# Outer weight sums of a seven-product matrix product: made by adding transfers instead of VectorE, with two waits and three signs moved

## What is computed

```
for i in 0, 1:
    x = x + 0.5 * swiglu_ffn(rmsnorm(x, n_ffn1[i]), ffn1_w_gu[i], ffn1_w_down[i])
    h = rmsnorm(x, n_mix[i])
    x = x + (gla_mixer(h, ...) if i == 0 else pool_mixer(h, ...))
    x = x + mem_cross_attn(rmsnorm(x, n_xattn[i]), rmsnorm(mem, n_mem[i]), x_w_q[i], x_w_kv[i], x_w_o[i])
    x = x + 0.5 * swiglu_ffn(rmsnorm(x, n_ffn2[i]), ffn2_w_gu[i], ffn2_w_down[i])
return rmsnorm(x, n_final)

def swiglu_ffn(h, w_gu, w_down):          # w_gu 1024 x 5632, w_down 2816 x 1024
    g, u = jnp.split(h @ w_gu, 2, axis=-1)
    return (jax.nn.silu(g) * u) @ w_down
```

## Time and profile before

| | us |
|---|---|
| median of 3 runs | 1940.71 (1940.7 to 1941.51) |
| the profiled execution | 1940.65 |
| its span, from first to last instruction | 1938.9 |
| TensorE matmul busy | 1926.8 (99%), 12020 matmuls |
| VectorE busy | 1411.2 (73%) |
| ScalarE busy | 963.9 (50%) |
| POOL busy | 161.6 (8%) |
| transfers in all | 215.01 MB, 111 GB/s |

### The profile page before, as it was taken

The page is one execution under the profiler, slowest core; times in us unless marked ns, Lnnn a source line. Parts: engine busy times, 40 slices in busy tenths (PEclk is TensorE's granted clock), DMA queues, the critical chain, the costliest instruction groups (busy, mean ns, idle before and its releaser), DMA issues.

```text
span 1938.9 us, 31412 instructions
## 1 busy us (share of the span) xinstructions
PE 1926.8 (99%) x12020; PEld 1742.0 (90%) x12020; DVE 1411.2 (73%) x2173; ACT 963.9 (50%) x1612; POOL 161.6 (8%) x199
## 2 busy tenths in 40 slices
PE   9999999999999999999999999999999999999998
PEld 7998997888898889989998998899898889989997
DVE  7865985577765659947976995698487669937964
ACT  7542554356564546524553653356256446524543
POOL 2000001100102210000001000000312121200000
PEclk9999999999999999999999999999999999999999
DMA  6333334323434633333333333333353424443332
GB/s 181 87 100 107 108 91 129 117 66 109 126 114 120 184 87 109 103 103 99 98 102 107 94 99 105 101 109 103 105 179 124 109 69 114 114 160 109 109 98 87
DMA packets 293830, 215.01 MB, mean 111 GB/s; under 512 B 23539, under 2 KB 276593, under 8 KB 293729
## 3 DMA queue, kind: packets, MB, share of 16 engines
q1 hardware_dynamic: 270112, 192.96, 33.3%
q0 software_dynamic: 6368, 17.63, 3.4%
q10 hardware_dynamic: 17248, 3.16, 0.8%
HBM read 203.23 MB, written 10.49 MB: 110 GB/s over the span
## 4 chain that ended last, share of the span: by engine, by line
PE 95%; DVE 2%; ACT 2%; issue 1%; ACTq 0%; DMA 0%; DVEq 0%
PE ps L418 18%; PE ps L419 18%; PE ps L420 18%; PE ps L995 13%; PE ps L996 13%; PE ps L997 13%; ACT w_hi L1376 1%; DVE w_lo L2056 1%; ACTq L1755 0%; PE ps L855 0%; PE ps L921 0%; DVE sums L2809 0%; DMA x_tok<-in_x 0%; ACT h_hi L1376 0%; DVE x L2346 0%
## 5 line engine op out<-in xcount | busy, mean ns | idle before, releaser
L2056 DVE TENSOR_TENSOR w_lo<-raw,w_hi 128x512 fp32r<-128x512 f32 (+5 forms) x367 | 402.4, 1097 | 254.9 <-ACT w_hi L1376 254.3
L1376 ACT ACTIVATE w_hi<-raw 128x512 fp32r<-128x512 f32 (+5 forms) x367 | 341.4, 948 | 265.2 <-PE ps L420 253.0
L995 PE MATMUL ps<-s_hi,w_hi 128*128 128x256 f32 x1248 | 353.8, 283 | 0.1
L997 PE MATMUL ps<-s_hi,w_lo 128*128 128x256 f32 x1248 | 353.2, 283 | 0.0
L996 PE MATMUL ps<-s_lo,w_hi 128*128 128x256 f32 x1248 | 353.2, 283 | 0.0
L996 PE MATMUL ps<-h_lo,w_hi 128*128 128x256 f32 x936 | 264.9, 283 | 0.0
L997 PE MATMUL ps<-h_hi,w_lo 128*128 128x256 f32 x936 | 264.9, 283 | 0.0
L995 PE MATMUL ps<-h_hi,w_hi 128*128 128x256 f32 x936 | 264.8, 283 | 0.0
L1376 ACT ACTIVATE w_hi<-w_sums 128x512 fp32r<-128x512 f32 x312 | 187.5, 625 | 138.9 <-DVE w_sums L2088 69.4
L995 PEld LDWEIGHTS ps<-s_hi,w_hi 128*128 128x128 f32 x1248 | 239.5, 192 | 0.9 <-issue 0.5
L996 PEld LDWEIGHTS ps<-s_lo,w_hi 128*128 128x128 f32 x1248 | 239.6, 192 | 0.0
(11 more groups left out here) (395 smaller groups left out, 3433.8 us busy)
## 6 DMA issues: line engine op xcount, KB each, us to landing
raw<-in_ffn_w_gu SPq DMA_DIRECT2D x172, 512.0 KB, 5.1
raw<-in_ffn_w_down SPq DMA_DIRECT2D x36, 768.0 KB, 4.5
raw<-in_x_w_kv SPq DMA_DIRECT2D x16, 1024.0 KB, 6.0
raw<-in_ffn_w_down SPq DMA_DIRECT2D x24, 640.0 KB, 4.2
raw<-in_gla_w_in SPq DMA_DIRECT2D x12, 1024.0 KB, 5.2
raw<-in_x_w_q SPq DMA_DIRECT2D x8, 1024.0 KB, 5.1
raw<-in_x_w_o SPq DMA_DIRECT2D x8, 1024.0 KB, 6.3
raw<-in_gla_w_out SPq DMA_DIRECT2D x8, 512.0 KB, 3.4
```

What stands on the lines that cost most here:

```text
L995: nc.tensor.matmul(to, hi[:, kk, :], right_hi, start=fresh, stop=False, skip_group_check=True)
L997: last = nc.tensor.matmul(to, lo[:, kk, :], right_hi, start=False, stop=kk == KH - 1, skip_group_check=True)
L1376: return nc.scalar.activation(out_ap, in_ap, ACT.Copy, **kw)
L2056: return nc.vector.tensor_tensor(out_ap, value, hi.bitcast(F32), ALU.subtract)
```

## The change

1. **Outer sums.** In each run, the slots from the third on (62 of 78) no longer get their outer sums from VectorE. SyncE loads the first summands into the place of the sums, and POOL issues one transfer of 512 KB with `accum_op=add` that adds the second summands from memory. The up block of the second half of the input features still goes to `raw`, that of the first half no longer does; so a slot is loaded by four transfers (512, 256, 256, 256 KB) and one that adds (512 KB). The sums have two buffers, by even and odd place in the run. `sum_three` and the high parts of P5 and P7 wait for the adding transfer.
2. **Signs.** Adding transfers only add, so the forms become sums of unchanged blocks, and the signs go into the sums of x and into `seed_fourth` and `high_up`.
3. **Stores.** `memory_store` moves from ScalarE to POOL, ahead of `add_squares(1)`.
4. **Norm copy.** `sum_x(0, 1)` moves behind `spread_rms(0)` and the two first gate products.

```
# SyncE, load_ffn, ahead of the two loads as they were
+ if w in mixed_slots and by_transfer(mixed_slots.index(w)):          # in_run[m] >= 2
+     m = mixed_slots.index(w)
+     sp.wait_ge(*form_lo_count(m - 2, P7))
+     sp.dma_start(raw[:, w % 2, :, 0:P], both[:, :, 0, s * P:(s + 1) * P])\
+       .then_inc(raw_loaded[w % 2], 16)
+     for g in range(2):
+         sp.dma_start(outer_sums[in_run[m] % 2][:, g], both[:, 0:KH, g, s * P:(s + 1) * P])\
+           .then_inc(raw_loaded[w % 2], 16)
+     sp.dma_start(raw[:, w % 2, KH:, P:], both[:, KH:, 1, s * P:(s + 1) * P])\
+       .then_inc(raw_loaded[w % 2], 16)
+     continue
# POOL
+ def memory_store():                       # the same eight transfers as before on ScalarE
+ def add_outer(n, part, l):
+     m, s = mixed_first[n, part] + l, l + (PLAIN_FIRST[n], HALF)[part]
+     w = mixed_slots[m]
+     up = (io.ffn1_w_gu, io.ffn2_w_gu)[n % 2][n // 2].rearrange("(k p) (g n) -> p k g n", p=P, g=2)[:, :, 1, :]
+     pool.wait_ge(raw_loaded[w % 2], loaded[w])
+     if transfers_before(m) > 0:
+         pool.wait_ge(sig.outer_added, 16 * transfers_before(m))
+     pool.dma_start(outer_sums[l % 2][:].rearrange("p h k n -> p (h k) n"), up[:, :, s * P:(s + 1) * P],
+                    accum_op=ALU.add).then_inc(sig.outer_added, 16)
+ def add_run(n, part):
+     for l in range(2, mixed_count(n, part)):
+         add_outer(n, part, l)
...
+ add_run(0, 0); add_run(0, 1)              # before the wait for the end of FFN 0's runs
  pool.dma_start(mem_tok[:], ...)
+ memory_store()
  add_squares(1)
...                                         # add_run(1, .) and (2, .) around add_squares(4), (3, 1) at the end
  turn_x: for m in range(C):
+     if m + 2 < mixed_count(3, 0):
+         add_outer(3, 0, m + 2)
# ScalarE, form_hi
- if i in SUM_OF:
-     act.wait_ge(sig.w_sum_ready, OPENED + 3 * m + SUM_STEP[i])
+ if i in (P5, P7) and by_transfer(m):
+     act.wait_ge(sig.outer_added, 16 * (transfers_before(m) + 1))
+ elif i in SUM_OF:
+     act.wait_ge(sig.w_sum_ready, sum_count(m, SUM_STEP[i]))
# ScalarE, ffn
- if (n, part, pair) == (0, 1, 1):
-     memory_store()
# VectorE
  sum_columns(m):  dve.wait_ge(raw_loaded[w % 2], loaded[w])
+                  if by_transfer(m): return
-     nc.vector.tensor_tensor(w_sums[:, 0:2], *outer_columns(w), ALU.subtract)
+     nc.vector.tensor_tensor(outer_sums[in_run[m] % 2][:], *outer_columns(w), ALU.add)
  sum_three(m):
+     if by_transfer(m):
+         dve.wait_ge(sig.outer_added, 16 * (transfers_before(m) + 1))
  seed_fourth:
- nc.vector.tensor_tensor(ps[:, d, 0:TH], ps[:, b, 0:TH], sq[:, s % 2, TH:], ALU.add)
+ nc.vector.scalar_tensor_tensor(ps[:, d, 0:TH], ps[:, b, 0:TH], -1.0, sq[:, s % 2, TH:], ALU.mult, ALU.subtract)
...                                         # high_up and the second sum of x in the same way
  opening:
      x_sums_lo(0, 0)
- sum_x(0, 1)
      spread_rms(0)
      ...                                   # the two first gate products
+ sum_x(0, 1)
```

More of the change, by code:

```diff
@@ L102, in place_ffn @@
                 else:
-                    if s in (PLAIN_FIRST[n], HALF):
+                    first = (PLAIN_FIRST[n], HALF)[part]
+                    if s == first:
                         mixed_first[n, part] = len(mixed_slots)
-                    place(("gu", n, s), 0, 0, C, mixed=True, loads=2)
+                    in_run.append(s - first)
+                    place(("gu", n, s), 0, 0, C, mixed=True, loads=2 if s - first < 2 else 4)
             if n == 3:
@@ L183, in mixed_end, with by_transfer, transfers_before, sum_count @@
         return mixed_first[n, part] + mixed_count(n, part)
+    def by_transfer(m):
+        return in_run[m] >= 2
+    def transfers_before(m):
+        return sum(by_transfer(i) for i in range(m))
+    def sum_count(m, step):
+        return OPENED + 3 * m - transfers_before(m) + step - int(by_transfer(m))
     def first_of_run(m):
@@ L454, in form_source @@
             if i in SUM_OF:
-                return w_sums[:, SUM_OF[i], :, :]
+                m, which = mixed_slots.index(w), SUM_OF[i]
+                return outer_sums[in_run[m] % 2][:, which] if which < 2 else inner_sums[:, which - 2]
             return quarter(w, int(i != P1), int(i == P3))
@@ L712, in load_o @@
                                    o_scratch[n].rearrange("t (c p) s -> c p t s", c=2)[c]).then_inc(sig.o_loaded, 16)
+            def memory_store():
+                columns_of = mem_scratch.rearrange("(b i) t -> i b t", i=32)
+                for mt in range(MT):
+                    pool.wait_ge(sig.blocks_ready, mt + 1)
+                    for a in range(4):
+                        tokens_of = slice(mt * P + 32 * a, mt * P + 32 * (a + 1))
+                        pool.dma_start(columns_of[:, :, tokens_of],
+                                       mem_blocks[32 * a:32 * (a + 1), mt, :].rearrange("i (b j) -> i b j", j=32))\
+                            .then_inc(sig.mem_stored, 16)
+            def add_outer(n, part, l):
[10 more added lines that the diff above has]
+                    add_outer(n, part, l)
             row = 0
@@ L752, in _ @@
             pool.dma_start(mem_cols[1][:], mem_scratch.rearrange("(c p) t -> p c t", p=P)).then_inc(sig.mem_loaded, 16)
+            add_run(1, 0)
+            add_run(1, 1)
             add_squares(4)
+            add_run(2, 0)
+            add_run(2, 1)
             bands()
@@ L1746, in memory_scale @@
                                          scale=mem_rms[:, mt:mt + 1]).then_inc(sig.mem_scaled, 1)
[L1748 to L1757, removed]
             def memory(i):
@@ L2101, in sum_four @@
                         dve.wait_ge(sig.x_sum_step, OPENED + 16 * (n + 1))
-                nc.vector.tensor_tensor(w_sums[:, 3], quarter(mixed_slots[m], 1, 0), w_sums[:, 2], ALU.subtract)\
+                nc.vector.tensor_tensor(inner_sums[:, 1], quarter(mixed_slots[m], 1, 0), inner_sums[:, 0], ALU.add)\
                   .then_inc(sig.w_sum_ready, 1)
@@ L2116, in sum_x @@
                 dve.wait_ge(sig.x_sum_step, OPENED + step + 1)
-                nc.vector.tensor_tensor(x_sums[:, 1, :], x_sums[:, 0, :], x_scaled[:, low], ALU.subtract)\
-                  .then_inc(sig.x_sum_step, 1)
+                nc.vector.scalar_tensor_tensor(x_sums[:, 1, :], x_sums[:, 0, :], -1.0, x_scaled[:, low],
+                                               ALU.mult, ALU.subtract).then_inc(sig.x_sum_step, 1)
                 dve.wait_ge(sig.x_sum_step, OPENED + step + 3)
                 nc.vector.scalar_tensor_tensor(x_sums[:, 3, :], x[:, kk + KH, low], gain(f, kk + KH), x_sums[:, 1, :],
-                                               ALU.mult, ALU.subtract).then_inc(sig.x_sum_step, 1)
+                                               ALU.mult, ALU.add).then_inc(sig.x_sum_step, 1)
             def x_sums_lo(f, kk):
@@ L2164, in seed_fourth @@
                         dve.wait_ge(sig.mixed_dve_step, dve_step(m - 1, C12_TAKEN))
-                    nc.vector.tensor_tensor(ps[:, d, 0:TH], ps[:, b, 0:TH], sq[:, s % 2, TH:], ALU.add)\
-                      .then_inc(sig.mixed_dve_step, 1)
+                    nc.vector.scalar_tensor_tensor(ps[:, d, 0:TH], ps[:, b, 0:TH], -1.0, sq[:, s % 2, TH:], ALU.mult,
+                                                   ALU.subtract).then_inc(sig.mixed_dve_step, 1)
                 def low_gate(m, s):
@@ L2179, in high_up @@
                         dve.wait_ge(sig.mixed_dve_step, dve_step(m - 2, GATED))
-                    nc.vector.tensor_tensor(sq[:, s % 2, 0:TH], ps[:, b, 0:TH], sq[:, s % 2, TH:], ALU.add)\
-                      .then_inc(sig.mixed_dve_step, 1)
+                    nc.vector.scalar_tensor_tensor(sq[:, s % 2, 0:TH], ps[:, b, 0:TH], -1.0, sq[:, s % 2, TH:], ALU.mult,
+                                                   ALU.subtract).then_inc(sig.mixed_dve_step, 1)
                 def low_gated(m, s):
```

24 lines of the change are left out of this document (16 added, 8 removed).

## The result

| | before | after |
|---|---|---|
| median, us | 1940.89 (1940.7 to 1941.51) | **2031.35** (2023.17 to 2034.7) |
| ratio to before | | 1.0461 [1.0445, 1.0477] |
| profiled execution, its span | 1940.65, 1938.9 | 2034.7, 2032.9 |

Forecast were 1934.3 us and, 8 times in 10, 1931.5 to 1962. The change costs 90 us instead of giving back 6: the wrong sign by far, and outside the range. First the page after: the busy times, the granted clock in 40 slices, and two of the transfer queues (packets, MB, share of 16 engines' span).

The account below looks back on a forecast made before the run. TensorE, busy 1926.8 of 1938.9 us at full clock, was taken to bound the kernel. Savings of 1.25 + 4.1 + 1.0 = 6.35 us from 1940.65 gave 1934.3 us; 8 in 10, 1931.5 to 1962.

Parts of the forecast that it names:

- When it lands: Each slot's adding transfer: lands 5.1 us after issue (ends 4.3 to 7.6), at 819.3, in time by 0.3 us.
- 12.2 free: In each slot: time from the first load's issue (807.48) to the deadline for the adding transfer's landing (819.65).
- the prediction's own price: Adding transfers past the deadline: lateness e stretches two slots by e, so 62 slots cost 31 us per us.
- rival (a): Third sums from a run's third slot on: adding transfers land late, 1950 to 1965 us, middle 1957; chance 0.32.
- the stores: Around 336 us: POOL issuing memory's stores removes TensorE's stall (2.5 us) and lower-clock matmuls (1.64 us), 4.1 us together.
- its bound of 7.6 us: Adding transfer's landing: upper end, from another POOL transfer of 1024 pieces; e = 2.2 would cost 68 us.
- its 1.25 us: First run of the last FFN: relieving VectorE of outer sums removes the matmuls' lag, -1.25 us.
- rival (d): VectorE's wait in the third sum replaces the outer sum; 1.25 us stay, 1935.6 us; chance 0.55 jointly with the forecast.
- rival (c): Around 336 us: POOL's stores and following adds replace ScalarE's wait; 4.1 us stay, 1938.4 us; chance 0.06.
- The norm copy: In the opening: moved ahead of four sums of x, it removes TensorE's wait for the first gate product, -1.0 us.
- The signs: Seed, high up product and a sum of x become scalar_tensor_tensor: at most 0.06 us more each, off the path, 0.

Follow-up runs that it names:

- e3: The changed kernel with POOL's transfer as a plain copy of the same 512 KB, without the addition: 1970.51 us, ratio 1.0151.
- d2: e9 with eight small POOL fills ahead of each adding transfer, holding the chain for 2.0 us: 1979.54 us, ratio 1.0198.
- e5: The changed kernel with adding transfers only in every other slot from the third on (35 instead of 62): 2012.61 us, ratio 1.0368.
- e2: The changed kernel with every outer sum on VectorE again, no adding transfers; signs and both moves kept: 1936.13 us, ratio 0.9974.
- e4: The changed kernel, outer loads issued first once their buffer is free, POOL waiting for them alone: 1934.81 us, ratio 0.9967; again 1934.37, 0.9965.
- e1: The kernel before with only the two moves, memory's stores on POOL and the norm copy ahead of x sums: 1936.26 us, ratio 0.9975.
- e10: e4 with adding transfers only in the first run of the last FFN (7 of 62): 1935.09 us, ratio 0.9970.
- e9: The changed kernel, loads issued when they were but the two outer loads first, POOL waiting for those alone: 1936.04 us, ratio 0.9973.
- e9b: e9 with the old load order, 512 KB of raw first, POOL still waiting for the outer loads alone: 1981.66 us, ratio 1.0209.
- d1: e9 with three small POOL fills ahead of each adding transfer, holding the chain for 0.8 us: 1940.33 us, ratio 0.9996.
- e7: The changed kernel with VectorE making outer sums; the 62 adding transfers still go, onto a buffer nobody reads: 1936.06 us, ratio 0.9973.

## Why the prediction was wrong

**The step that failed: "When it lands".** The issue-to-landing time of the adding transfer was taken as 5.1 us, "close to the nearest row, half of the second read hidden behind the first". It is 6.45. The nearest row was 0.5 us short for a copy (e3: 4.8 against 4.3). The term for the addition was worked out as 1.6 us and came out as 1.65 (6.45 - 4.8), and I had halved it for no reason that a row gave. Unhalved, the sum from the rows would have had 5.9, late by 0.5 and some 16 us dearer. That the second read is what takes the 1.65 us is not shown.

The prediction quoted the Trainium skill ("Collectives: The Full Stack", Part 3), which says of the reduce step of collectives that a transfer which adds is slowed by its second source read. By that rule the landing would have been at 5.9 us: late by 0.5, and the rival as the forecast. The measurement lies above 5.9, and on the rule's side.

**What the step left out.** The chain was 6.6 + 0.1 + 5.1 = 11.8 us against 12.2 free. At 6.45 it would be 13.2, late by 1.0, and by the prediction's own price 31 us dearer. The loss was 99. Three things more:
- The loads overlap the addition of the slot before. The 6.6 us to their last landing was right for the first such slot (6.5), and 8.7 and 7.4 for the next two. With its own 0.3 POOL issues after 8.1 us on average, where the prediction had 6.7, and the chain is 14.6 us, 2.4 late. At 31 us per us this is 74 us, and the gaps are 83; in d2 (13.3 on average, 1.1 late) it is 34, and the gaps are 40. So the price nearly held, and what was mis-sized is the lateness: 1.35 us for the addition and 1.4 for POOL's start. About 1.0 of the 1.4 is the overlap, since POOL starts after 7.1 us in e5, where no transfer runs beside the loads.
- The third slot of a run has only 11.0 to 11.8 us: gaps of 1.9 to 2.5 us there in seven of the eight runs, and of 6.6 in the one where the adding transfer took 9.7 us.
- Eight of the 61 stalls, those of 2.3 us and more, were followed by a stretch at the lower clock, with matmuls 0.21 us apart instead of 0.12: about 13 us. The prediction had counted just that for the stores (1.64 us) and not for its own rival (a). None of the other 53 brought one; the first matmuls behind the gaps at full clock cost about 5 us besides.

**Rival (a)** named the place, the waiting instruction and the side, and the chance of 0.32 was too small; its "1950 to 1965" took the landing up to 6.4 us, which was right, and left the rest of the chain in its best case. The range failed for the same reason: its bound of 7.6 us for the landing was worth 68 us by the prediction's own price, and I did not carry it into the range. Even that would have ended near 2002, 29 us short.

**What held.** VectorE's outer sum was off the path: with VectorE making all of them (e2) nothing is lost in seven of the eight runs. In the first run of the last FFN its 1.25 us come back when the transfers are in time (e4), so rival (d) fell. The stores gave 4.3 us for 4.1, with a clock of 1.00 after them, so POOL's cover (rival (c)) was enough. It was thin, though: in the profiled executions of e1, e2 and e10 TensorE still waits 0.6 us for a low part at that place, and the stretch gives 3.5 us. The norm copy gave 0.7 for 1.0: TensorE's wait is gone, and the first run begins 0.72 us earlier. In other kernels with the same opening it begins 0.4 to 1.5 us earlier, so a single execution doesn't fix this term. The signs cost nothing (e2 against e1).

**What the cause is.** POOL waited for all four loads of the slot, though its transfer reads none of two of them, and the two that it needs were issued second and third. Shown: with the same transfers and both faults mended the loss is 2 us (e9), with the order left as it was 47 (e9b), and a delay put back in front of POOL's transfer brings the loss back (d1, d2). Without the addition it is 38 (e3), and the traffic alone costs 2 us at most (e7, e9).

## What to carry to other kernels

When a step is handed to a transfer that follows on other transfers, write down its whole chain at the slot's own pace, with its neighbour's transfer running beside it, and hold it against the free time of the first iterations too, not of a middle one only. Let it wait on its own semaphore for just what it reads, and issue that first: here this was worth 95 us at no cost. A price for lateness also has to carry what comes behind the stalls: here 17.7 us on top of 83.1, most of it at the lower clock, which followed the longest stalls alone.

## What the runs showed of the hardware

- An adding transfer of 512 KB is not a copy with an addition. In the plain copy the 62 transfers are 15680 - 6752 = 8928 packets (144 each; e1's POOL queue has 6752), with the addition 71232 - 6752 = 64480 (1040 each), for the same 51.19 MB in the queue. By the shares of the queue they hold the 16 engines for (0.093 x 1970.6 - 0.037 x 1934.5)/62 = 1.8 us each as a copy and (0.166 x 2032.9 - 0.037 x 1934.5)/62 = 4.3 us with the addition. POOL is held 1.54 us by the issue instead of 0.88. How much of the 1.65 us is the second read, the smaller packets or the longer issue was not separated.
- While POOL's transfer is under way, SyncE's own issues can take far longer. The fourth load of a slot (L560), in the changed kernel, in e3 with plain copies, and in e5, where no transfer runs beside it:

```profile
L560 SPq DMA_DIRECT2D raw<-in_ffn_w_gu x62: 498/1110/2380, 58.1 to 1938.9; - x62
...
L560 SPq DMA_DIRECT2D raw<-in_ffn_w_gu x62: 498/1310/2837, 58.2 to 1877.1; - x62
...
L560 SPq DMA_DIRECT2D raw<-in_ffn_w_gu x35: 368/548/953, 57.3 to 1921.1; - x35
```

  Its median is 1.1 and 1.3 us with a transfer beside it and 0.55 without, so the addition is not the reason.
- Some stalls in a stretch that is otherwise full were followed by the lower level of TensorE's clock (1.2 GHz), others were not. In the changed kernel it followed all eight stalls of 2.3 to 6.6 us and none of the other 53, the longest of which was 2.2 us. In e5 it also followed some of 1.9 to 2.3 us, and in d2 one of 2.7 us was not followed by it. The granted clock was 0.83 in the ten us after the stall of 2.4 us shown above, and 0.92 over the whole first run of the last FFN. These are the windows around a stall of 2.1 us (from 207.8 to 209.8) that was not followed by it:

```profile
208.00:211.50 3.50, 1.65 (x13) 1.66 (x14) 3.34 (x7) 2.53 (x5) 0.00 (x0) 1.00 1.17 309
211.50:221.50 10.00, 9.22 (x77) 9.04 (x76) 7.16 (x15) 5.24 (x11) 1.52 (x1) 1.00 0.81 159
```

  In e9 and e4 both runs shown stay at 1.00.
